# A hybrid attention and retention step: attention's opening work done inside the input map, group norms eight slots earlier, PSUM evacuations given to ScalarE

## The reference

```python
h = _modulate(_rmsnorm(x, norm_mix), shift, scale)
cq, ckv, kr, rq, rk, rv, rg, ga, gb = _split(h @ w_in, IN_SIZES)
# branch A, 8 heads of attention: softmax(q k^T / sqrt(96)) v
s = einsum(qn, k_nope) + einsum(qr, k_rope)
p = softmax(s * scale);  attn = einsum(p, v)
# branch B, 4 heads of retention in both directions, then a group norm per head
lg = log_sigmoid(decay_logit)
sc = einsum(qc, kc) * dmat;  y = sc @ vc + (qc * q_dec) @ S
S_new = S * c_dec + (kc * k_dec)^T vc
mu = mean(y);  var = mean((y - mu)**2)
ret = silu(rg) * ((y - mu) * rsqrt(var + EPS)) * gn
# both branches, gated, then a product-key expert layer and a norm
x = x + g1 * ((sigmoid(ga) * (attn @ w_up_a) + sigmoid(gb) * (ret @ w_up_b)) @ w_o)
x = x + g2 * peer(modulate(rmsnorm(x)))
y = rmsnorm(x)
```

## Time and profile before

| what | us |
|---|---|
| median of 3 runs (lowest, highest) | 2238.37 (2236.64, 2243.58) |
| the profiled execution, time | 2247.16 |
| the profiled execution, span of the core | 2245.3 |
| PE busy | 2121.4 (94%) |
| DVE busy | 1803.1 (80%) |
| ACT busy | 1246.4 (56%) |
| attention block, first matmul to last `attend` | 350.71 to 526.62 |

### The profile page before, as it was taken

How to read it: one execution, slowest core, us unless ns; L and a number is a source line. 1 busy time by engine, 2 the same in 40 slices (tenths; PEclk the granted TensorE clock), 3 DMA queues, 4 the chain that set the end, 5 groups by cost and what they waited for, 6 DMA issues and landing times. The chain is left out here.

```text
span 2245.3 us, 33445 instructions
## 1 busy us (share of the span) xinstructions
PE 2121.4 (94%) x12006; PEld 1166.2 (52%) x12006; DVE 1803.1 (80%) x3656; ACT 1246.4 (56%) x1678; POOL 433.7 (19%) x408
## 2 busy tenths in 40 slices
PE   6999996988789999999999999999999999999997
PEld 4667674555556754445555554544444444444443
DVE  4466636776777757889999999945899999999999
ACT  4555763455667635624444447768465565565562
POOL 0011110000111300223323232410223223223220
PEclk7999997998999999999999999999999999999998
DMA  7885751005667844778989998895888788788772
GB/s 293 329 312 162 224 203 57 29 19 216 215 207 263 303 159 159 240 252 261 355 303 341 319 355 310 324 370 220 334 298 322 292 300 319 292 302 321 291 276 75
DMA packets 193675, 573.86 MB, mean 256 GB/s; under 512 B 18784, under 2 KB 52352, under 8 KB 186368
## 3 DMA queue, kind: packets, MB, share of 16 engines
q1 hardware_dynamic: 113872, 323.99, 42.0%
q0 software_dynamic: 48704, 173.04, 20.7%
q10 hardware_dynamic: 30960, 75.07, 8.6%
HBM read 455.03 MB, written 117.00 MB: 255 GB/s over the span
## 5 line engine op out<-in xcount | busy, mean ns | idle before, releaser
L306 PE MATMUL mrg_ps<-h_hi,lin_hi 128*128 128x512 f16 (+1 forms) x1376 | 462.0, 359 | 2.8 <-DVE h_lo L639 2.8
L306 PE MATMUL mrg_ps<-h_lo,lin_hi 128*128 128x512 f16 (+1 forms) x1376 | 462.0, 359 | 0.0
L306 PE MATMUL mrg_ps<-h_hi,lin_lo 128*128 128x512 f16 (+1 forms) x1376 | 461.7, 358 | 0.0
L288 DVE SCALAR_TENSOR_TENSOR lin_lo<-lin_raw,lin_wsc,lin_hi 128x1024 f16<-128x1024 f32 x132 | 169.2, 1282 | 147.2 <-ACT lin_hi L282 147.0
L2074 POOL DMA_INDIRECT row<-v_dram,picked x128 | 177.8, 1389 | 558.3 <-DVE acc L2716 437.0
L2138 POOL DMA_INDIRECT row<-u_rows_dram,picked x128 | 176.1, 1376 | 472.0 <-DVE dot_junk L2324 354.0
L282 ACT ACTIVATE lin_hi<-lin_raw,lin_wsc 128x1024 f16<-128x1024 f32 x132 | 151.1, 1146 | 198.7 <-DVE lin_wsc L143 155.0
L2586 PE MATMUL ps_w<-oh_turned,oh_buf 128*128 128x128 f16 x1024 | 224.3, 219 | 5.4 <-ACT region L2252 5.3
L306 PEld LDWEIGHTS mrg_ps<-h_hi,lin_lo 128*128 128x128 f16 x1376 | 135.3, 98 | 128.2 <-issue 1.4
L306 PEld LDWEIGHTS mrg_ps<-h_hi,lin_hi 128*128 128x128 f16 x1376 | 134.4, 98 | 120.4 <-issue 4.1
L2824 PE MATMUL y_ps<-region 128*128 128x512 f16 x512 | 194.7, 380 | 1.8 <-PEq L2078 1.8
(11 more groups left out here) (424 smaller groups left out, 4007.5 us busy)
## 6 DMA issues: line engine op xcount, KB each, us to landing
lin_raw<-w_all_dram SPq DMA_DIRECT2D x132, 512.0 KB, 6.1
act_scratch<-activated ACTq DMA_DIRECT2D x128, 256.0 KB, 4.5
wgt_scratch<-region ACTq DMA_DIRECT2D x64, 512.0 KB, 6.4
region<-v_dram SPq DMA_DIRECT2D x15, 2048.0 KB, 7.7
oh_buf<-v_dram SPq DMA_DIRECT2D x15, 2048.0 KB, 7.6
act_buf<-w_all_dram SPq DMA_DIRECT2D x38, 512.0 KB, 4.7
lin_hi<-split_scratch SPq DMA_DIRECT2D x64, 256.0 KB, 3.3
lin_lo<-split_scratch SPq DMA_DIRECT2D x64, 256.0 KB, 4.8
```

Source lines behind the costliest of these rows:

```text
L288: nc.vector.scalar_tensor_tensor(out=self.lo[b][:], in0=self.raw[b][:], scalar=self.wsc[:, self.col(b)], in1=self.hi[b][:], op0=ALU.mult, ...
L306: last = nc.tensor.matmul(self.ps[b % 2][:, half, 0:ts.stop - ts.start], w_[:, kc, :], x_[:, kc, ts], start=(j == 0 and kc == 0), stop=(j ...
```

## The change

The PSUM tile `ps_n` outlives the input map, and its halves are the attention block's `pt` and `po`. The small tiles of the attention block (`negmax`, `den`, `rden`, `lgw`, `ksteps`) lie in `v_flat`; the turned values lie in `proj[:, 0:4]`, and the second set of probabilities, which lay there, gets a tile `prob1`. In the input map: the first logarithm step at VectorE's slab 18, its Exp at ScalarE's slab 20 ahead of the Silus, the transfer of `ksteps` at SP's slab 26, `decay_log` at VectorE's slab 27 (the 25 instructions of L1462 to L1481, moved word for word into a function), six turns at TensorE's slabs 27 to 32 with VectorE's copies at 28 to 33, totals at 30 and scales at 31, context scores at 33 and 34, their maxima at 35.

```diff
@@ input map, ACT slab
                             if (q, b) == (gq, 0):
+                                act.wait_ge(s("lg_abs"), 1)
+                                nc.scalar.activation(lgw[:, 1, :], lgw[:, 0, :], ACT.Exp, scale=-1.0).then_inc(s("lg_exp"), 1)
                                 for h in range(RH):
@@ input map, DVE prepare
+                            if sl == 18:
+                                dve.wait_ge(s("kh_rope"), 2 * HEADS)
+                                x = cols[:, C_LOG:C_LOG + 8]
+                                link(nc.vector.tensor_scalar(lgw[:, 0, :], x, -1.0, None, ALU.mult))
+                                nc.vector.tensor_tensor(lgw[:, 0, :], lgw[:, 0, :], x, ALU.max).then_inc(s("lg_abs"), 1)
+                            if sl == 27:
+                                decay_log()
+                            if 28 <= sl < 29 + NT:
+                                k = sl - 28
+                                dve.wait_ge(s("turned3"), k + 1)
+                                nc.vector.tensor_copy(rv_tok[:, k, :] if k < NT else rk_tok, ps_n[:, k % 2, :]
+                                                      ).then_inc(s("turned3_read"), 1)
...
+                            if sl == 31:
+                                dve.wait_ge(s("att_total"), 1)
+                                dve.wait_ge(s("ret_total"), 1)
+                                act_scale(dve, link, 1, att_total, "att_scaled")
+                                act_scale(dve, link, 2, ret_total, "ret_scaled")
+                            if sl == M_END - 1:
+                                for u in range(CTX):
+                                    dve.wait_ge(s("ctx_scores"), u + 1)
+                                    nc.vector.tensor_reduce(negmax[:, u, :], ps_n[:, u, :].rearrange("p (i n) -> p i n", i=4),
+                                                            AX.X, ALU.max, negate=True).then_inc(s("ctx_maxed"), 1)
@@ input map, PE prepare
+                            if 27 <= sl < 28 + NT:
+                                k = sl - 27
+                                pe.wait_ge(s("v_read"), NALL // P)
+                                if k >= 2:
+                                    pe.wait_ge(s("turned3_read"), k - 1)
+                                for h in range(RH):
+                                    src = proj[:, M_RV + h, k * P:k * P + P] if k < NT else proj[:, M_RK + h, 0:P]
+                                    last = nc.tensor.transpose(ps_n[:, k % 2, h * P:h * P + P], src, ident[:])
+                                last.then_inc(s("turned3"), 1)
+                            if sl == 30:
...
+                                total_pe(pe, "ret", ret_total, 2, RH, "bound", 1)
+                            if sl in (33, 34):
+                                u = sl - 33
+                                pe.wait_ge(s("turned3_read"), NT + u)
+                                for k in range(4):
+                                    h = 4 * u + k
+                                    last = nc.tensor.matmul(ps_n[:, u, k * P:k * P + P], q_h[0:QK, h, 0:NCTX], k_h[0:QK, h, 0:NCTX],
+                                                            start=True, stop=True)
@@ attention block
-                            [proj[:, k, :] for k in range(4)]]
+                            [prob1[:, k, :] for k in range(4)]]
...
+                    def kept_by_act(u, k=0):
+
+                        return u < UNITS - 3 or (u + k) % 2 == 0
...
-                    def var_head(u, k):
-                        return u - CTX - 4 if k == 1 and 0 <= u - CTX - 4 < RH else None
-
-                    def mean_head(u, k):
-                        return u - CTX - 3 if k == 4 and 0 <= u - CTX - 3 < RH else None
+                    def head_in(u, k, first):
+
+                        h, late = divmod(5 * (u - CTX) + k - first, NT)
+                        return h if late == 0 and 0 <= h < RH else None
+                    MEAN, VAR = 11, 13
@@ attention block, DVE body
-                            if turn_at(u, k) % 2:
+                            if not kept_by_act(u, k):
                                 evacuate(u, k)
...
-                            if k == 2 and 0 <= h < RH:
+                            if (h := head_in(u, k, VAR + 2)) is not None:
```

More of the change, by code:

```diff
@@ L654, in build @@
                 ckv = sb(keep, "ckv", [P, NALL])
+                ps_n = pb(keep, "ps_n", [P, 2, 512])
+                CTX, UNITS = 2, 2 + HEADS
+                v_rest = v_flat[:, V_END:V_END + 2 * N]
+                small = v_flat[:, V_END + 2 * N:7 * N + PAST]
+                negmax, den, rden = (small[:, 4 * UNITS * k:4 * UNITS * (k + 1)].rearrange("p (u k) -> p u k", k=4) for k in range(3))
+                lgw = small[:, 12 * UNITS:12 * UNITS + 64].rearrange("p (w n) -> p w n", n=8)
+                lg = lgw[:, 7, :]
+                ksteps = small[:, 12 * UNITS + 64:12 * UNITS + 64 + 2 * RH]
+                rv_tok = proj[:, 0:4, :].rearrange("p k n -> p (k n)").rearrange("p (k n) -> p k n", k=NT)
+                rk_tok = ckv[:, 0:512]
                 q_h = x_t
@@ L1261, in _ @@
                     def _(sp):
-                        for dst, name in ((steps[0], "steps0"), (steps[1][:], "steps1"), (ksteps[:], "ksteps"), (state[:], "state"),
+                        for dst, name in ((steps[0], "steps0"), (steps[1][:], "steps1"), (state[:], "state"),
                                           (inv_e, "inv_k"), (rel[0], "rel0"), (rel[1], "rel1"), (twice, "twice")):
@@ L1454, in _ @@
                         invert(1)
-                        maximum(CTX, 0)
-                        maximum(CTX, 1)
-                        for k in range(2, NT + 1):
-                            turned(k)
                         invert(CTX, 0)
                         invert(CTX, 1)
-                        dve.wait_ge(s("lg_exp"), 1)
-                        link(V.tensor_scalar(lgw[:, 2, :], lgw[:, 1, :], 2.0, None, ALU.add))
-                        link(V.reciprocal(lgw[:, 3, :], lgw[:, 2, :]))
@@ L1507, in body @@
                                 invert(u + 1, k - 1)
-                            h = u - CTX - 4
-                            if k == 1 and 0 <= h < RH:
+                            if (h := head_in(u, k, VAR)) is not None:
                                 dve.wait_ge(s("gn_var"), h + 1)
@@ L1666, in ret_values @@
                             last.then_inc(s("ret_av"), 1)
-                        score(0)
-                        score(1)
-                        turn(0)
-                        turn(1)
-                        score(CTX, 0)
-                        score(CTX, 1)
-                        for k in range(2, NT + 1):
-                            turn(k)
-                        score(CTX, 2)
-                        score(CTX, 3)
+                        for j in range(4):
+                            score(CTX, j)
                         turn_probs(0)
                         turn_probs(1)
-                        pe.wait_ge(s("exp"), CTX)
-                        nc.tensor.matmul(totals[:, 0:NALL // P], ones[:], hsum[:, 1, 0:NALL // P], start=True, stop=True
-                                         ).then_inc(s("att_total"), 1)
-                        total_pe(pe, "ret", totals[:, 8:8 + RH], 2, RH, "bound", 1)
-                        pe.wait_ge(s("att_scaled"), 1)
-                        pe.wait_ge(s("ret_scaled"), 1)
                         attend(0)
```

179 lines of the change are left out of this document (70 added, 109 removed).

## The result

The change makes the kernel slower: 2251.11 us against 2243.46 of the kernel before (medians of 10 executions each), ratio 1.0037, 95% interval 1.0027 to 1.0048, that is 6 to 11 us. The forecast was 2236.5 with 0.56 on "no difference that can be told"; the time lies over the upper end of the range, 2248. Of the 14.6 us between forecast and time 5.1 lie in the base: the forecast put its sum on 2238.37, the median of three executions of the kernel before, and the median of ten, with these three among them, is 2243.46.

What follows compares the result with a forecast made beforehand. TensorE bounds the input map and units 3 to 6; elsewhere it waits on VectorE or ScalarE. Input map +5.3, prologue −13.3, slots +6.2 sum to −1.8 on 2238.37: 2236.5 us, range 2222 to 2248.

Steps and rivals of the forecast that it cites:

- copies, not placed: In the slots: 1.0 us added for ScalarE's copies that now wait behind exponents and roots, assigned to no unit.
- the price of the passes in the map: In the input map: added transposes, context scores and totals cost 4.7 us, all on a TensorE without slack.
- the Exp and its table load: At slab 20 of the input map: 1.28 us of table load and 0.21 of instruction on ScalarE, 1.5 taken as paid.
- 2.7 was worked out: Unit 5: TensorE waits 2.7 us at the third score, since the output instructions delay the maximum and exponent before it.
- rival 3: Input map: its waits and missing slack hide most new matmuls, so it costs 1.5; total −5.6 us, 2232.8; chance 0.15.
- rival 1: Units 5 to 7: VectorE's lateness fits the slack of two score tiles; total −16.9 us, 2221.5; chance 0.25.
- The wait for the square behind slab 20: In the input map: TensorE's wait for ScalarE's square, 0.3 us before, would be near 1.8.
- nearer the warm end: Prologue: taken as 18.5 us, between 17.5 by the stepped chain and 20.2 at half clock, saving 13.3.
- the half-clock end of the working: Prologue: at half clock the chain's matmuls add 2.7 us, giving 20.2 and a saving of 11.6.
- rival 2: Units 5 to 7: waits at k = 0 cool TensorE, 2.2 us more per unit; total +10, 2248.4; chance 0.15.
- 3.5 us of wait: Units 5 to 7: the wait length from which TensorE's clock would fall; the forecast's own count was 0.8 short.
- two passes fewer: Unit 8: TensorE loses two mean and variance passes of 1.07 us each, but ScalarE's 14.95 mostly stays; −1.7.

Runs made afterwards that it cites:

- open_only: The changed kernel with group norms and copies both as before, leaving only the prologue's move into the input map; 0.9973 of the kernel before.
- no_chain: The changed kernel with four of the five output instructions of each group norm left out; 0.9983 of the kernel before.

## Why the prediction was wrong

Means over the four traces of the change and the two of before, stage by stage:

| stage | forecast | measured | where it comes from |
|---|---|---|---|
| input map | +5.3 | +6.3 | +5.5 at full clock, as counted; 1.5 more in two of four, clock 0.99 |
| prologue | −13.3 | −11.6 | clock 0.50 to 0.61: 19.76 each time; 30.8 in the second trace of before |
| unit 2 | −0.7 | −1.0 | as forecast |
| unit 3 | 0 | +0.8 | clock 0.84 in one of four |
| units 4, 5, 6 | +2.1, +3.7, +1.6 | +2.2, +4.3, +3.0 | at full clock +2.2, +3.9, +1.8 |
| unit 7 | +2.8 | +4.2 | wait of 3.64 and clock 0.78 to 0.85 in all four |
| unit 8 | −1.7 | +0.4 | the output chain of head 3, overlooked |
| unit 9 | −2.6 | −1.3 | −2.7 in the trace at full clock |
| copies, not placed | +1.0 | not seen | units 4 to 6 at full clock come out without them |
| sum | −1.8 | +7.3 | timed: +6 to +11 |

The sum misses by 9.1: 6.3 in the slots (+12.5 where +6.2 was forecast), 1.7 in the prologue and 1.0 in the map. The mechanisms of the forecast are there with their prices at full clock: the price of the passes in the map, of the Exp and its table load, the wait of 2.55 where 2.7 was worked out, and rival 3 (a hidden map) and rival 1 (an absorbed chain) are ruled out by it. The wait for the square behind slab 20 is 1.82 in the first trace, as the forecast named it (1.8). For the Exp the row decided rightly against the price in the Trainium skill (ScalarE: Activation LUTs, "What ACT_TABLE_LOAD costs"): about 2.7 us for a change of set by the page, 1.5 with the instruction by the run that moves it. Two steps of the sum failed, and its base was low.

The first is TensorE's clock. The sum priced units 3 to 7 and 9 at full clock and took the prologue "nearer the warm end because the input map ends at full clock". But TensorE idles 3.7 us between the blocks and again in the prologue, which ran at 0.50 to 0.61 in all four traces, and took 19.76, by the half-clock end of the working (20.2); with the higher clock of `open_only` it took 18.8, by the forecast's 18.5. In the units it was rival 2 that described what happens, and it had 0.15. Its +10 stands near the measured 6 to 11. Its 2.2 per unit, for which it shows no working, lies between what a fall of the clock cost (1.7 in two units of the third trace, 3.2 in two of the fourth). What was wrong was its point of decision, "3.5 us of wait", drawn from one row of before, with shorter waits priced at nothing. In unit 7 the wait was 3.64, past that point, in all four traces, and the clock was low each time. But the waits of 2.55 in units 5 and 6 were followed by a lower clock too, in three cases of eight, and that of 1.8 to 2.0 in the map in two of four. A mechanism that strikes in a part of the executions belongs in the sum with that part, not in a rival below a threshold.

The second is the step on unit 8, "two passes fewer", −1.7 where +0.4 was measured: by the slots of the change (output at 15 + 5h) head 3's chain falls on unit 8's k = 0, where it stands ahead of VectorE's copy of the next turn, k = 1. TensorE waits 3.07 us for that copy in all four traces. The forecast took the passes out of unit 8 and gave the chain's wait to units 5 to 7 alone; without the chain unit 8 takes 16.2 (`no_chain`), 4.1 less than in the first trace, part of it by the clock.

The base was low: the median of three executions, 2238.37, lies 5.1 us under the median of ten. With the ten as base the range would have ended near 2253 and the time would have lain in it, so that the time falls outside the range is owed to the base; that the change is slower and not level is owed to the two steps above. The forecast was right not to take the profiled execution of before, 2247.16, for the kernel: its opening was 5.8 us longer than in the second trace. The two first traces alone would have shown a loss of 3.4 in the stages and none in the position of the next block.

What stays open: by the traces the stages explain 7.3 us, by the timing the change costs 6 to 11, with 8 in the middle. Whether the rest, if there is one, lies in how often the clock falls (four traces are few) or in the later blocks, where one trace of four had 3 us more, was not settled. Nor does any run show what decides whether the clock falls behind a given wait.

## What to carry to other kernels

Work moved ahead of a busy TensorE stage has to be placed by engine and place in the cycle, not by the time at which its data is ready: the means and variances stood eight slots earlier and the outputs seven, but the output held VectorE ahead of a maximum on which TensorE's next score depended, and most of the 3.5 us that can be left out came through (waits of 2.55, 2.55 and 3.64). A wait of TensorE costs its length and, in a part of the executions, a stretch of half clock behind it (1.5 to 3.2 us here); both belong in the sum. One trace is one draw of the clock, and three timed executions are a weak base for a change of 0.3%: where a stage's busy time differs at equal counts, take another before comparing.

## What the runs showed of the hardware

The granted clock behind an idle stretch isn't settled by its length: with the same program and the same idle stretch of 2.55 us, TensorE stayed at full clock in unit 5 in three traces and fell to 0.93 over the unit in one; in unit 6 it fell in two of four. In the map it fell behind waits of 1.96 and 1.83 us and held behind 1.82 and 1.92. A table load on ScalarE, taken out of a chain that TensorE waits for, gave back 1.5 us together with its small instruction (1.28 and 0.21 in the trace of `open_only`, the instruction starting 1.29 after the load), with no further gap.
